# Norm sums by strips inside the panels, the per-token product behind the mixer, MLP row panels two later, post-norm updates by quarters

## What is computed

```python
for layer in range(2):
    x = x + 0.5 * swiglu(rmsnorm(x, norm_ffn1), ffn1_gate, ffn1_up, ffn1_down)     # 1024 -> 2816 -> 1024
    x = x + hybrid_mixer(rmsnorm(x, norm_mix), ...)                                # w_in, HGRN2, gated delta, RG-LRU, w_out
    x = x + 0.5 * swiglu(rmsnorm(x, norm_ffn2), ffn2_gate, ffn2_up, ffn2_down)
x = rmsnorm(x, norm_final)
h = x
u = rmsnorm(h, g_pre_mix)                                                          # w_in: retention and dilated attention
h = h + rmsnorm(mixed @ w_o, g_post_mix)
h = h + rmsnorm(square(relu(rmsnorm(h, g_pre_mlp) @ w_up)) @ w_down, g_post_mlp)
gate = sigmoid(rmsnorm(h, g_pre_ple) @ w_ple_gate + b_ple_gate)
h = h + rmsnorm(gate * (p @ w_ple_in), g_post_ple)
```

## Time and profile before

| | us |
|---|---|
| median of 3 runs (1914.05 to 1917.64) | 1914.84 |
| the profiled execution's own time | 1914.54 |
| its span, first to last instruction | 1912.7 |
| TensorE busy | 1794.1 |
| VectorE busy | 1090.4 |
| ScalarE busy | 917.1 |
| GpSimd busy | 176.9 |
| mean granted TensorE clock | 0.977 |

### The profile page before, as it was taken

How to read it: one execution, slowest core, us unless ns; L and a number is a source line. 1 busy time by engine, 2 the same in 40 slices (tenths; PEclk the granted TensorE clock), 3 DMA queues, 4 the chain that set the end, 5 groups by cost and what they waited for, 6 DMA issues and landing times.

```text
span 1912.7 us, 34097 instructions
## 1 busy us (share of the span) xinstructions
PE 1794.1 (94%) x15120; PEld 1729.0 (90%) x15120; DVE 1090.4 (57%) x1231; ACT 917.1 (48%) x966; POOL 176.9 (9%) x120
## 2 busy tenths in 40 slices
PE   8999987899999999999789999999999989899997
PEld 7999987799999999998779999889897779899986
DVE  6544788464446544688556445654465456655555
ACT  6343674453345334476444344544444454544444
POOL 0000071000000000052000000774000000000000
PEclk9999998899999999999899999999999999999999
DMA  7555442135555555453035555456254514445541
GB/s 258 177 184 191 144 134 88 46 122 186 178 183 169 177 178 193 148 162 117 19 102 176 178 187 187 142 186 206 93 170 160 176 39 162 138 159 191 180 160 39
DMA packets 206530, 290.99 MB, mean 152 GB/s; under 512 B 4560, under 2 KB 170576, under 8 KB 206128
## 3 DMA queue, kind: packets, MB, share of 16 engines
q1 hardware_dynamic: 205936, 287.04, 46.3%
q0 software_dynamic: 448, 1.77, 0.3%
HBM read 287.75 MB, written 1.05 MB: 151 GB/s over the span
## 4 chain that ended last, share of the span: by engine, by line
PE 81%; DVE 9%; ACT 5%; issue 2%; POOL 2%; DMA 0%; SPq 0%; ACTq 0%; DVEq 0%
PE colb L788 52%; PE acc L788 26%; PE aux L788 2%; DVE w_lo L1527 2%; ACT w_hi L1177 2%; POOL arena L657 1%; DVE arena L1732 1%; DVE u L1587 1%; DVE x L1630 1%; DVE u L1645 1%; DMA raw<-ffn_gate 0%; DVE op_lo L1593 0%; POOL arena L658 0%; ACT arena L1490 0%; DVE arena L1790 0%
## 5 line engine op out<-in xcount | busy, mean ns | idle before, releaser
L1527 DVE TENSOR_TENSOR w_lo<-raw,w_hi 128x2048 fp32r<-128x2048 f32 x271 | 626.0, 2310 | 591.1 <-ACT w_hi L1177 590.5
L1177 ACT ACTIVATE w_hi<-raw 128x2048 fp32r<-128x2048 f32 x271 | 515.8, 1904 | 414.2 <-PE acc L788 230.7
L788 PE MATMUL colb<-u_hi,w_lo 128*128 128x256 f32 x2256 | 295.7, 284 | 5.7 <-DVE w_lo L1527 5.7
L788 PE MATMUL colb<-u_hi,w_hi 128*128 128x256 f32 x2256 | 298.1, 285 | 1.7 <-ACT u_hi L1287 0.9
L788 PE MATMUL colb<-u_lo,w_hi 128*128 128x256 f32 x2256 | 295.0, 284 | 0.0
L788 PEld LDWEIGHTS colb<-u_hi,w_lo 128*128 128x128 f32 x2256 | 282.3, 193 | 6.5 <-DVE w_lo L1527 6.5
L788 PEld LDWEIGHTS colb<-u_hi,w_hi 128*128 128x128 f32 x2256 | 283.4, 193 | 3.1 <-issue 1.5
L788 PEld LDWEIGHTS colb<-u_lo,w_hi 128*128 128x128 f32 x2256 | 282.2, 193 | 0.0
L788 PE MATMUL acc<-op_hi,w_hi 128*128 128x256 f32 x1328 | 203.9, 286 | 12.4 <-ACT op_hi L1299 8.1
L788 PE MATMUL acc<-op_hi,w_lo 128*128 128x256 f32 x1328 | 201.0, 284 | 0.2
L788 PE MATMUL acc<-op_lo,w_hi 128*128 128x256 f32 x1328 | 200.4, 284 | 0.0
(11 more groups left out here) (298 smaller groups left out, 1725.6 us busy)
## 6 DMA issues: line engine op xcount, KB each, us to landing
raw<-w_in SPq DMA_DIRECT2D x78, 1024.0 KB, 5.1
raw<-ffn_gate SPq DMA_DIRECT2D x44, 1024.0 KB, 5.3
raw<-ffn_up SPq DMA_DIRECT2D x44, 1024.0 KB, 5.3
raw<-ffn_down SPq DMA_DIRECT2D x44, 1024.0 KB, 4.9
raw<-w_up SPq DMA_DIRECT2D x16, 1024.0 KB, 5.4
raw<-w_down SPq DMA_DIRECT2D x16, 1024.0 KB, 5.0
raw<-w_out SPq DMA_DIRECT2D x8, 1024.0 KB, 4.9
raw<-w_ret_out SPq DMA_DIRECT2D x8, 1024.0 KB, 4.9
```

The costliest lines, as they stand in the source:

```text
L788: return pe.matmul(o, a, b, start=start, stop=stop, skip_group_check=True)
L1177: act.activation(split_view(w_hi, r), raw[:, p % RAW_SLOTS, 0:r["kt"] * r["nc"]], ACT.Copy)\
L1527: tt(split_view(w_lo, r), raw[:, p % RAW_SLOTS, 0:r["kt"] * r["nc"]], split_view(w_hi, r).bitcast(F32), ALU.subtract).then_inc(sem("w_lo_r ...
```

## The change

- **Strip sums.** At a seam (all but the first) the 8 ones-matmuls in front of the first early panel go. Behind that panel 8 matmuls with 32 columns of ones sum the squares, dealt to four groups of 32 partitions of `aux` in turn; ScalarE copies the 128 x 256 result into `rstd`; one full ones-matmul, inside the second early panel behind its 20th matmul, adds the groups up (`parts`, `parts_sum`).
- **High parts first.** ScalarE makes the high part straight from x with the gain as scale, two instructions per quarter; DVE makes the low part from x, gain and high part, two per quarter, after all updates. u32 isn't written there any more. DVE's split of the first early panel comes after quarter 0. ScalarE splits the second early panel before the squares of quarters 1 to 3, the third after the table load.
- **Pass order.** The first early panel and the third panel run high x high, weights' low, then operand's low.
- **Fill.** One fill of four quarters in the first early panel's step, behind the split of the third panel: u32 = x * gain * rstd, two DVE instructions per quarter.
- **Per-token product.** p has its own SBUF tile and is loaded early. p @ w_ple_in is a panel of a new kind behind w_o, into the three colb banks and aux; ScalarE copies it to SBUF, and `ple` reads it there.
- **MLP rows.** Row panel i runs after up panel i+2.
- **Post-norm.** `x_update("post")` makes two tiles of u32 and adds them, quarter by quarter.

```diff
@@ schedule of the second block
+                if i == 3:
+                    p_op = operand(p32[:, :, :].rearrange("p a b -> p (a b)"), [("p_loaded", 16)])
+                    step("op_hi", r=p_op)
+                    step("op_lo", r=p_op)
                 row_gemm_panel(ap["w_o_2"][0], i, rs[i], i == 0, i == 3)
+            p_op["panel"] = len(panels)
+            resident(ap["w_ple_in_2"][0], op_tiles(p_op), [("op_ready", p_op["r"] + 1)], ple_e)
...
-            todo = None
+            todo = []
             for i in range(16):
                 panel(kpn(ap["w_up_2"][0])[:, :, i * PC:(i + 1) * PC], KD, PC, "A", u_op,
                       [("u_ready", 4 * f)], by="act", evac=("relu", len(ops)))
                 step("relu2", r=len(ops), evac=n_act)
-                if i == 1:
-                    step("op_hi", r=todo)
-                    step("op_lo", r=todo)
-                if i:
-                    row_gemm_panel(ap["w_down_2"][0], i - 1, todo, i == 1, False)
-
+                if i >= 2:
+                    row_gemm_panel(ap["w_down_2"][0], i - 2, todo.pop(0), i == 2, False)
                 r = operand(hid[:, len(ops) % 2, :], [("hid_ready", i + 1)] + [("panel_used", len(panels) + 1)] * (i == 0))
-                todo = r
-                if i:
-                    step("op_hi", r=r)
-                    step("op_lo", r=r)
-            row_gemm_panel(ap["w_down_2"][0], 15, todo, False, True)
-            p_op = operand(p32.rearrange("p a b -> p (a b)"), [("p_loaded", 16)])
-            step("op_hi", r=p_op)
-            step("op_lo", r=p_op)
+                todo.append(r)
+                for o in todo if i == 1 else [r] if i else []:
+                    step("op_hi", r=o)
+                    step("op_lo", r=o)
+            row_gemm_panel(ap["w_down_2"][0], 14, todo.pop(0), False, False)
+            row_gemm_panel(ap["w_down_2"][0], 15, todo.pop(0), False, True)
@@ tensor engine
+                elif r["kind"] == "P":
+                    pe.wait_ge(sem("w_lo_ready"), p + 1)
+                    pe.wait_ge(sem("op_ready"), op_ready)
+                    for i, o in enumerate([colb[:, (r["c"] + i) % 3, :] for i in range(3)] + [aux[:, :]]):
+                        if i < 3:
+                            col_bank_free(pe, r["c"] + i - 3)
+                        else:
+                            pe.wait_ge(sem("rstd_ready"), r["norm"])
+                        for m in range(2):
+                            for kk in range(2):
+                                xh, xl = r["xop"](kk)
+                                for part in range(3):
+                                    last = mm(o[:, T * m:T * m + T], (wh, wh, wl)[part][:, kk, 2 * P * i + P * m:2 * P * i + P * m + P],
+                                              (xh, xl, xh)[part], m == 0 and kk == 0 and part == 0, kk == 1 and part == 2)
+                        if i < 3:
+                            last.then_inc(sem("p_bank"), 1)
...
-                    for part in range(3):
+                    for part in (0, 2, 1) if r.get("gained") or r.get("fresh") else (0, 1, 2):
                         if part == 2:
                             pe.wait_ge(sem("w_lo_ready"), p + 1)
                         for kk in range(r["kt"]):
                             xh, xl = r["xop"](kk)
+                            if part == 1 and kk == 2 and r.get("half") == 1 and r["norm"] > 1:
+                                parts_sum(r)
...
+                if r.get("gained") and r["norm"] > 1:
+                    parts(r)
+
+            def parts(r):
+
+                pe.wait_ge(sem("sq_ready"), 4 * r["norm"])
+                for kk in range(KD):
+                    g = slice(32 * (kk % 4), 32 * (kk % 4) + 32)
+                    last = mm(aux[g, 0:T], ones[:, 0:32], sq[:, kk, :], kk < 4, kk >= 4)
+                last.then_inc(sem("norm_parts"), 1)
+
+            def parts_sum(r):
+
+                pe.wait_ge(sem("parts_copied"), r["fill"]["n"] - 1)
+                mm(aux[:, T:2 * T], ones, rstd[:, :]).then_inc(sem("norm_summed"), 1)
@@ scalar engine
+                def high(b):
+                    chunk(b)
+                    if b == 3:
+                        act.wait_ge(sem("panel_used"), r["panel"])
+                    for t in range(2):
+                        ins = act.activation(gained_chunk(op_hi, r["op"], b)[:, t, :], x[:, 2 * b + t, :], ACT.Copy,
+                                             scale=c(r["gain"], r["at"] + 2 * b + t))
+                    ins.then_inc(sem("g_hi_ready"), 1)
...
+                high(0)
+                square(0)
+                for b in (1, 2, 3):
+                    high(b)
+                split_hi_to(r["panel"] + 1)
+                for b in (1, 2, 3):
+                    square(b)
                 ln_exp_tables()
+                split_hi_to(r["panel"] + 2)
+                act.wait_ge(sem("norm_parts"), r["fill"])
+                act.activation(rstd[:, :], aux[:, 0:T], ACT.Copy).then_inc(sem("parts_copied"), 1)
                 act.wait_ge(sem("norm_summed"), r["n"])
-                rstd_from(rstd[:, :], aux[:, 0:T], 1.0 / D).then_inc(sem("rstd_ready"), 1)
-
-            def fill(r, half):
-                for i in (2 * half, 2 * half + 1):
+                rstd_from(rstd[:, :], aux[:, T:2 * T], 1.0 / (32 * D)).then_inc(sem("rstd_ready"), 1)
@@ vector engine
+                while n_lo[0] <= min(p, n_panels - 1) and not panels[n_lo[0]].get("gained"):
...
-            def x_gained(r, b):
-
-                for i in (2 * b, 2 * b + 1):
-                    ins = ts(u32[:, i, :], x[:, i, :], c(r["gain"], r["at"] + i), None, ALU.mult)
-                ins.then_inc(sem("xg_ready"), 1)
-
             def g_lo_(r, b):
                 dve.wait_ge(sem("g_hi_ready"), 4 * (r["n"] - 1) + b + 1)
-                s = slice(2 * b, 2 * b + 2)
-                tt(gained_chunk(op_lo, r["op"], b), u32[:, s, :], gained_chunk(op_hi, r["op"], b).bitcast(F32), ALU.subtract).then_inc(sem("gained"), 1)
+                hi, lo = gained_chunk(op_hi, r["op"], b), gained_chunk(op_lo, r["op"], b)
+                for t in range(2):
+                    ins = stt(lo[:, t, :], x[:, 2 * b + t, :], c(r["gain"], r["at"] + 2 * b + t), hi[:, t, :].bitcast(F32),
+                              ALU.mult, ALU.subtract)
+                ins.then_inc(sem("gained"), 1)
 
             def gained(r):
-
                 for b in range(4):
                     if r["nx"] == 0:
                         dve.wait_ge(sem(f"x_loaded{b}"), 16)
+                        g_lo_(r, b)
                     else:
                         update[0](b)
-                    x_gained(r, b)
-                    if b:
-                        g_lo_(r, b - 1)
-                g_lo_(r, 3)
-                if r["nx"] == 0:
-                    split_lo_to(0)
-
-            def fill(r, half):
-
+                    if b == (0 if r["nx"] else 3):
+                        split_lo(panels[n_lo[0]])
+                        n_lo[0] += 1
+                if r["nx"]:
+                    for b in range(4):
+                        g_lo_(r, b)
+
+            def fill(r):
                 dve.wait_ge(sem("rstd_ready"), r["norm"])
                 dve.wait_ge(sem("panel_used"), r["panel"])
-                for i in range(2 * half, 2 * half + 3):
-                    if i < 2 * half + 2:
-                        s = slice(2 * i, 2 * i + 2)
-                        tt(u32[:, s, :], u32[:, s, :], bc(rstd[:, :], 1, 2), ALU.mult).then_inc(sem("u32_ready"), 1)
-                    if i > 2 * half:
-                        dve.wait_ge(sem("u_hi_ready"), 4 * (r["n"] - 1) + i)
-                        s = slice(2 * i - 2, 2 * i)
-                        tt(u_lo[:, s, :], u32[:, s, :], u_hi[:, s, :].bitcast(F32), ALU.subtract).then_inc(sem("u_ready"), 1)
+                for i in range(4):
+                    for kk in (2 * i, 2 * i + 1):
+                        ins = stt(u32[:, kk, :], x[:, kk, :], c(r["gain"], r["at"] + kk), rstd[:, :], ALU.mult, ALU.mult)
+                    ins.then_inc(sem("u32_ready"), 1)
+                for i in range(4):
+                    dve.wait_ge(sem("u_hi_ready"), 4 * (r["n"] - 1) + i + 1)
+                    s = slice(2 * i, 2 * i + 2)
+                    tt(u_lo[:, s, :], u32[:, s, :], u_hi[:, s, :].bitcast(F32), ALU.subtract).then_inc(sem("u_ready"), 1)
...
+                        if r["kind"] == "post":
+                            for i in (2 * b, 2 * b + 1):
+                                ins = stt(u32[:, i, :], acc[:, T * i:T * i + T], c(r["gain"], i), rstd[:, :], ALU.mult, ALU.mult)
+                            normed[0] += 1
+                            ins.then_inc(sem("acc_normed"), 1)
+                            dve.wait_ge(sem("acc_normed"), normed[0])
...
-                    tt(g, g, bank[b], ALU.mult).then_inc(sem("gated_ready"), 1)
+                    tt(g, g, ple_e[:, 2 * b:2 * b + 2, :].rearrange("p a b -> p (a b)"), ALU.mult)\
```

(1 more changed line is left out.)

107 lines of the change are left out of this document (68 added, 39 removed).

## The result

The changed kernel takes **1899.74 us** (median of 4 runs, 1899.33 to 1900.33) beside 1914.44 for the one before (4 runs, 1912.90 to 1917.64) on the same chip: ratio 0.9921, 95% interval 0.9909 to 0.9933. Its profiled execution took 1899.87 us with a span of 1897.9, 14.8 less than before, at the same mean granted clock (0.978, before 0.977).

The account below looks back on a forecast made before the run. TensorE was taken as the bound, busy 1794.1 of 1912.7 us. Seam terms 2.9 - 6.5 - 5.7 - 0.4 - 2.7 - 1.2 = -13.6 from 1914.5 gave 1901.0 us; range 1891 to 1912, the forecast's own 1896 to 1906.

Parts of the forecast that it names:

- plain seams: Five steps from last row panel to next block's first panel, two to a mixer, three to an FFN; 5.7 and 6.5 won.
- FFN seam: Plain seam leading to an FFN, three of them; gain 2.15 us each, 6.5 in all.
- mixer: Plain seam leading to a mixer, two of them; gain 2.85 us each, 5.7 in all.
- N3: Third panel at a seam, behind the two early ones; to wait 0.3 us for its last high part.
- N4: Fourth panel at a seam; its weights ready 0.5 us late at an FFN seam, in time at a mixer's.
- E1: First early panel at a seam, raw product scaled afterwards; at plain seams first pass ends at +2.3 instead of +1.9.
- loss at the start: First seam: single fill comes behind DVE's split of N3, so first row panel is later; loss 2.9 us.
- second block: Seam stepping to the second block, fill beside POOL's tables; gain 0.4 us, between 2 and a loss of 1.5.
- MLP: Seam to the second block's MLP: per-token product fills the wait for rstd, third up panel before first row panel; gain 2.7.
- gate product: Last seam: row panel and norm ahead of E1 go, E1 cold at first; gain 1.2 us.
- rival 1: Strips do not overlap: eight seams each pay 3.6 instead of 1.2 us, giving 1920.5 us, slower; chance 0.08.
- price for two groups: If only two strips overlap, each seam pays 0.85 us more, giving 1908 us; chance 0.09.

Follow-up runs that it names:

- start and N4 edited: Changed kernel with VectorE's fill ahead of its split of N3 at the start, and everywhere ScalarE's split of N4 right behind the fill's high parts: 1895.05 us.

## Why the prediction was right, point by point

**Right.** 1901.0 was forecast, 1899.74 measured, inside the forecast's own range; the sum was 13.6, the traces say 14.8. The plain seams came out as walked: gain 2.15 per FFN seam (2.19), 2.85 per mixer (2.81 and 2.83), by the mechanism named, with waits in N3, N4 and the row panel of 0.44, 0.46 and 0.36 for 0.3, 0.5 and 0.3. Two small errors offset each other in E1: its first pass took 2.68 and not 2.3, the strips 1.0 and not 1.2. The loss at the start is 3.1 for 2.9, from the cause named (shown by undoing it). The row panel stands at 40.50 for 40.45. The plain seams and the start together: 9.3 forecast, 9.1 measured (5.6 + 6.6 - 3.1). The rest was forecast at 4.3 and measured at 5.7, and there the sum's closeness is in part luck: the second block is 1.8 short, MLP and gate product are 2.3 over, and 0.9 came from the mixers, where nothing was forecast.

**Strips.** Four do run at once, which the half arrays of the earlier trace rows had let one expect. There the Trainium skill, TensorEngine Tiling (Array Packing), section Tiling Modes, warned of draining at a change of mode; the set costs 1.00 us including both changes, 0.2 more than a quarter of the 3.26 at full width, so no full tail of 0.16 per switch was paid. The prediction's price for two groups, 0.85 a seam, is right as well (0.88). What I did not see: that there is a way to do nearly as well without strips. The kernel with one full sum spends 3.3 us on it, about what serial strips would, and loses 0.4 at an FFN seam, because it has no copy and no collecting matmul in front of rstd, and N3, N4 and the row panel stop waiting. Strips one after the other, rival 1's own case, would also have these two; no run shows them.

**Mis-sized: the second block.** "Gain 0.4" was a loss of 1.4, at the lower bound. The step that failed is the fill beside POOL: I had it "longer" and gave it no price. It took 4.98 us for 3.26, and N4's split stood behind it. Taking POOL away from it gave 1.65 us back.

**Mis-sized: MLP and gate product.** 4.0 for 2.7 and 2.2 for 1.2. I charged 1.0 for a cold E1 in the MLP; its clock stayed at 1.00, with the product in the wait. That is not the product's doing alone, since with start and N4 edited E1 is cold behind the same product. E1's first pass ended at 1653.8, and that is the forecast's 1662.5 less the shift of 8.7; the pass behind it took 1.92. The first row panel waited 1.31 for 1.7. In the gate product E1 did run cold and was over at 1860.1, where 1873.5 less the shift of 12.7 is 1860.8; strips, sum and the waits in N3 and N4 then took 2.7 where I had charged 3.

**Not foreseen: 1.4 us inside the first mixer.** Before, TensorE waited 2.00 us there for the gates, and the gates' matmuls behind the wait ran at a low clock: their 16 records took 4.88 us, now 3.72 without a wait. Against these 3.2 stand 1.3 for a panel that now runs at low clock just before (its pass 3.34 us for 2.01), and 0.4 elsewhere in the mixer. The wait comes from GpSimd, one multiplication in the gates' chain, in the kernel before and in the changed one:

```profile
252.06 18.51 POOL L657 TENSOR_TENSOR arena<-arena 8x256 f32<-8x256 f32 x1
```

```profile
252.37 13.92 POOL L675 TENSOR_TENSOR arena<-arena 8x256 f32<-8x256 f32 x1
```

No edit was aimed at it, and the second profile of the changed kernel has 11.75 us at the same place, so it varies from execution to execution. This gain is luck as far as the forecast goes. The kernels with full sums and with two groups have 18.5 there again, and the wait of 2.0 with it.

## What to carry to other kernels

Before making a step shorter, look at what the next panel waits for: behind a seam the chain rstd, fill, scale, evacuation, split was late already, and moving one split up a queue (1.0 us a seam) was worth more than overlapping sixteen matmuls (0.4). Work without dependencies is best put into the wait for a norm, where it may also keep the clock up. When two halves of a job are joined, see at each place where it runs whether what now stands ahead of it has its own wait; here the start alone lost 3 us to it. Before a gain or a loss is explained in a stretch that no edit touched, look at the same stretch in a second profile of the same kernel.

## What the runs showed of the hardware

- Matmuls on different column groups overlap in proportion: 16 records of 256 columns take 3.26 us at full width, 1.88 in two groups, 1.00 in four. Each record lasts about 0.38 in all three cases; with four groups, four of them start within 0.02 us.
- VectorE's fill instructions (x times a column scalar times rstd, 256 columns) take 0.62 us instead of 0.41 while POOL computes (4.98 against 3.25 for eight).
- One GpSimd multiplication of 8x256 in the gates' chain lasts 11.7, 13.9, 16.3 or 18.5 us in the mixers, while VectorE works without a pause; others of its line last 0.73 (spans on GpSimd are rough). The fourteen profiles have 28 of the long ones. In all five with 18.5 us VectorE waits 4.2 for GpSimd and TensorE 2.0 for the gates; at none of the other 23 does TensorE wait. The five are the first mixer before, with two groups and with the old pass order, and both with full sums. That this wait is the cause of these mixers' longer stretches is read from the traces; no edit tested it.
- The granted clock halves (2.4 to 1.2 GHz) for some 3 to 10 us at a time, and in part behind the same waits in one variant and not in another. In the profiles it did so around the gates in the mixers (0.62 from 286 to 294 with the full sums, 0.79 in the changed kernel), in the dilated attention, and in E1 of the MLP. Each place costs 1.3 to 2.5 us. In the changed kernel's two profiles the last two places run at full clock (1.00 from 1243 to 1840); over its mixers the clock is what it was (0.90 and 0.89, before 0.89 twice). Each variant that shifts its panels by some microseconds meets others. What decides it was not settled. (By the Trainium skill, TensorE: Matmul & The Clock Gate, section What's actually happening, the chip's watch on TensorE runs on its own and does not start with the kernel; that would fit, and no run here tests it.) It is the likely reason why 1.0 us a seam, seen in each stretch, is only partly seen in a median.
